# Second layer rebuilt as a pipeline of 32 items, with projections of rounded parts

## The reference, cut to what matters

```python
def shared_kv(x, g_norm, w_kv, g_k):
    kv = rmsnorm(x, g_norm) @ w_kv
    k, v = jnp.split(kv, [KV_WIDTH], axis=-1)
    k = rmsnorm(k.reshape(b, s, SWA_KV_HEADS, SWA_HEAD_DIM), g_k)
    ...    # bands: each block of 128 rows sees itself and the block before

def swa_layer(x, g_norm, w_in, g_q, sinks, w_out, k_band, v_band, bias, mask):
    proj = rmsnorm(x, g_norm) @ w_in
    q, gate = jnp.split(proj, [SWA_Q_WIDTH], axis=-1)
    q = rmsnorm(q.reshape(b, nb, BLOCK, SWA_KV_HEADS, SWA_GROUP, SWA_HEAD_DIM), g_q)
    scores = jnp.einsum('bnqkgd,bnjkd->bnkgqj', q, k_band).astype(jnp.float32)
    scores = scores * (SWA_HEAD_DIM ** -0.5) + bias[None, None]
    scores = jnp.where(mask[None, :, None, None], scores, -jnp.inf)
    m = jnp.maximum(jnp.max(scores, axis=-1, keepdims=True), sink)
    p = jnp.exp(scores - m)
    p = p / (jnp.sum(p, axis=-1, keepdims=True) + jnp.exp(sink - m))
    o = jnp.einsum('bnkgqj,bnjkd->bnqkgd', p.astype(v_band.dtype), v_band)
    o = o.reshape(b, s, SWA_Q_WIDTH) * jax.nn.silu(gate)
    return x + o @ w_out
```

## Time and profile before

| what | value |
|---|---|
| median of three runs | 2690.94 us (2686.0 to 2691.65) |
| profiled execution: span | 2686.3 us |
| profiled execution beside the runs | 0.3 above the lowest, 4.6 below the median; no other time of it is given |
| TensorE busy | 2500.3 us, 93% |
| VectorE busy | 1077.8 us, 40% |
| ScalarE busy | 751.9 us, 28% |
| POOL busy | 211.1 us, 8% |
| first stage | 0 to 936.7 us |
| second stage | 936.7 to 1537.1 us |
| third stage | 1537.1 us to the end |

### The profile page before, as it was taken

The page is one execution under the profiler, slowest core; times in us unless marked ns, Lnnn a source line. Parts: engine busy times, 40 slices in busy tenths (PEclk is TensorE's granted clock), DMA queues, the critical chain, the costliest instruction groups (busy, mean ns, idle before and its releaser), DMA issues. The chain is left out here.

```text
span 2686.3 us, 32568 instructions
## 1 busy us (share of the span) xinstructions
PE 2500.3 (93%) x11482; PEld 1864.2 (69%) x11482; DVE 1077.8 (40%) x2949; ACT 751.9 (28%) x1960; POOL 211.1 (8%) x292
## 2 busy tenths in 40 slices
PE   6999999999899878999999789999999998799998
PEld 5867778677578735555555477777777675688877
DVE  4223122241231134444444234676676767211132
ACT  3121221212220022222222132444444534211131
POOL 0010000100100010000000000001010000000013
PEclk8999999999999988999999888999999999899999
DMA  3111111111261252000001121011111010311112
GB/s 127 49 51 61 39 55 49 51 45 53 78 229 63 74 178 96 9 8 8 8 8 39 44 74 49 26 36 40 55 39 39 25 36 9 113 48 47 47 71 94
DMA packets 77371, 152.32 MB, mean 57 GB/s; under 512 B 6392, under 2 KB 26040, under 8 KB 75584
## 3 DMA queue, kind: packets, MB, share of 16 engines
q1 hardware_dynamic: 66768, 130.65, 13.8%
q10 hardware_dynamic: 9616, 13.81, 1.5%
q0 software_dynamic: 864, 6.29, 0.6%
HBM read 124.46 MB, written 26.27 MB: 56 GB/s over the span
## 5 line engine op out<-in xcount | busy, mean ns | idle before, releaser
L91 PE MATMUL heads_p_ps<-ret_w_second_hi_sb,ret_hT_hi_sb 128*128 128x512 f32 x384 | 161.7, 421 | 1.1 <-DVE ret_w_second_lo_sb L465 1.1
L91 PE MATMUL heads_p_ps<-ret_w_second_lo_sb,ret_hT_hi_sb 128*128 128x512 f32 x384 | 149.9, 390 | 0.0
L91 PE MATMUL heads_p_ps<-ret_w_second_hi_sb,ret_hT_lo_sb 128*128 128x512 f32 x384 | 149.4, 389 | 0.0
L921 PE MATMUL swa_p_ps<-swa_w_o_sb,swa_oT_sb 128*128 128x512 f32 x256 | 118.2, 617 | 0.9 <-DVE swa_oT_sb L1316 0.9
L921 PE MATMUL swa_p_ps<-swa_w_g_sb,swa_xT_sb 128*128 128x512 f32 x256 | 114.4, 600 | 3.9 <-DVE swa_w_g_sb L1343 3.9
L2506 DVE TENSOR_TENSOR mrg_sig_sb<-mrg_b_ps,mrg_sig_sb 128x512 f32<-128x512 f32 x32 | 22.1, 690 | 235.9 <-PE mrg_b_ps L2362 235.9
L2362 PE MATMUL mrg_b_ps<-mrg_w_br_sb,mrg_yT_sb 128*128 128x256 f32 x512 | 115.5, 379 | 0.0
L91 PE MATMUL att_proj_ps<-br_w_second_hi_sb,br_hT_hi_sb 128*128 128x512 f32 x256 | 110.7, 432 | 2.7 <-DVE br_w_second_lo_sb L2008 2.7
L1161 ACT ACTIVATE swa_probs_sb<-swa_probs_sb,swa_max_neg_sb 128x256 f32<-128x256 f32 x128 | 63.4, 496 | 169.9 <-DVE swa_max_neg_sb L1294 169.9
L2362 PEld LDWEIGHTS mrg_b_ps<-mrg_w_br_sb,mrg_yT_sb 128*128 128x128 f32 x512 | 96.5, 190 | 13.6
L1970 ACT ACTIVATE br_x_sb<-br_x_sb,att_max_neg_sb 128x256 f32<-128x256 f32 (+7 forms) x128 | 97.8, 768 | 19.5 <-DVE att_max_neg_sb L2181 19.5
(11 more groups left out here) (393 smaller groups left out, 5830.8 us busy)
## 6 DMA issues: line engine op xcount, KB each, us to landing
early_w_kv_sb<-a_w_blocks SPq DMA_DIRECT2D x28, 1024.0 KB, 5.1
all_w_block_sb<-w_turns SPq DMA_DIRECT2D x12, 2048.0 KB, 9.0
ret_o_dram<-heads_o_gated_sb ACTq DMA_DIRECT2D x32, 256.0 KB, 2.4
ret_out_o_rows_sb<-ret_o_dram POOLq DMA_DIRECT2D x6, 1024.0 KB, 5.2
heads_v_sb<-x SPq DMA_DIRECT2D x8, 512.0 KB, 4.3
all_w_block_sb<-a_w_blocks SPq DMA_DIRECT2D x2, 2048.0 KB
ret_out_x_rows_sb<-x SPq DMA_DIRECT2D x8, 512.0 KB, 5.4
x_dram<-ret_out_x_rows_sb SPq DMA_DIRECT2D x8, 512.0 KB, 2.6
```

The costliest lines, as they stand in the source:

```text
L91: mm = pe.matmul(out, rows[a], w[b], start=(k == 0 and a + b == 0), stop=(k == KT - 1 and b == 1))
L921: mm = pe.matmul(bank[:, 0:cols.stop - cols.start], h[:, k, :], w[:, k, cols], start=(k == 0), stop=(k == KT - 1))
```

## The change

Only the second stage is written anew, with a small part of it moved into the first.

- Work is cut into 32 items: four turns (one quad of heads each) over eight tiles. An item has one projection of 512 columns, 256 for the queries and 256 for the gates of its four heads; `window_blocks` lays the weights out that way. Item n goes through step n+1 (norm), n+2 (scores, maxima, exponentials), n+3 (transposes, values) and n+4 (gate, transposes of the output). All steps are written out; there is no hardware loop.
- The projections use `products` with parts. So normed rows of all eight tiles are kept transposed in two parts (`hT`), made in an opening loop together with all keys and values (`k_all`, `v_all`). Weights are split by `split_high` (ScalarE) and `split_low` (VectorE); the first half of k has two buffers, the second half (`w_second`) one.
- The outputs are stored transposed to DRAM, item by item, loaded again per tile, split, and projected by 16 products of 512 columns, four of them in steps 32 to 35 and twelve after them.
- The gate is x(1 + tanh(x/2)), with the factor 1/2 in the output weights: one tanh on ScalarE and one operation on VectorE. The product of gate and output moves to POOL, and so does the sink's difference.
- In the first tile the half of the band that is masked is left out, so no mask has to be put in and out.
- The product of bucket table and one-hot matrix, and its store, are done in the first stage; the second loads the skewed form and VectorE reverses it with a negative step (`flip_bias`).

```diff
 # first stage
+                if t == 3:
+                    pe.wait_ge(rel_in, 48)
+                    pe.matmul(p_o0[0:SWA_HEADS, 0:EXT], rel, onehot, start=True, stop=True).then_inc(ext_mm, 1)
...
+            act.wait_ge(ext_done, 1)
+            act.dma_start(dram["ext"], ext).then_inc(ext_out, 16)
...
+                if t == 5:
+                    dve.wait_ge(ext_mm, 1)
+                    dve.wait_ge(rel_in, 48)
+                    dve.tensor_tensor(ext, p_o0[0:SWA_HEADS, 0:EXT], ext_mask, ALU.add).then_inc(ext_done, 1)
...
+            dve.wait_ge(ext_out, 16)
 # second stage, TensorE
+            def keys_values(t):
...
+                mm = products(pe, p_kv[t % 2][:, 0:KV_COLS], at_tile(hT, slice(t * P, (t + 1) * P)),
+                              lambda k: [part[:, k, :] for part in w_kv])
+            def project(n, ks):
+                turn, t = divmod(n, TILES)
+                if ks[0] == 0:
+                    at_least(pe, qn_done, n - 1)
+                    at_least(pe, gate_done, n - 1)
+                if t == 0:
+                    pe.wait_ge(w_lo, KT * turn + ks[-1] + 1)
+                mm = products(pe, p_proj[n % 2][:], at_tile(hT, slice(t * P, (t + 1) * P)), lambda k: turn_w(turn, k), ks)
...
+            for s in range(TILES + 2):
+                if s < TILES:
+                    rows(s)
+                if 1 <= s <= TILES:
+                    keys_values(s - 1)
+                if s >= 2:
+                    transpose_keys(s - 2)
+                if s in (5, TILES):
+                    project(s // TILES, range(KT))
+            for n in range(1, ITEMS + AHEAD):
+                def along(ks):
+                    if 2 <= n < ITEMS:
+                        project(n, ks)
+                    elif n >= ITEMS:
+                        output(n - ITEMS, ks)
+                if 2 <= n < ITEMS + 2:
+                    scores(n - 2)
+                along(range(0, 3))
+                if 3 <= n < ITEMS + 3:
+                    transpose_probs(n - 3)
+                along(range(3, 6))
+                if 3 <= n < ITEMS + 3:
+                    values(n - 3)
+                if n <= ITEMS:
+                    transpose_queries(n - 1)
+                if n >= 4:
+                    transpose_out(n - 4)
+                along(range(6, KT))
+            for m in range(AHEAD, len(outputs)):
+                output(m, range(KT))
 # second stage, VectorE, one step
+                if t == 0 and turn < QUADS:
+                    for k in range(HALF, KT):
+                        split_low(turn, k)
...
+                if n >= 4:
+                    norm_out(n - 4)
+                if n <= ITEMS:
+                    query_squares(n - 1)
+                    put_gate(n - 1)
+                if 2 <= n < ITEMS + 2:
+                    bias_max(n - 2)
+                if n <= ITEMS:
+                    norm_queries(n - 1)
+                if 3 <= n < ITEMS + 3:
+                    copy_probs(n - 3)
+                    row_sums(n - 3)
+                if HALF <= t and turn + 1 < QUADS:
+                    split_low(turn + 1, t - HALF)
 # second stage, SyncE
+            for n in range(ITEMS):
+                store_out(n)
+                if n >= LOADS:
+                    load_out(n - LOADS)
+                if n == TILES or n == 2 * TILES:
+                    sp.wait_ge(w_lo, KT * (n // TILES + 1))
+                    sp.dma_start(w_raw[:], kt_view(dram["swa_turns"][n // TILES + 1])).then_inc(w_in, 16)
```

More of the change, by code:

```diff
@@ new lines, in turn_w, with late_w, o_parts, keys_of @@
+        def turn_w(turn, k):
+            return [part[:, k % HALF, :] for part in (w_first[turn % 2] if k < HALF else w_second)]
+        def late_w(k):
+            return [part[:, k, BANK:] for part in hT]
+        def o_parts(t):
+            cols = slice(t % 4 * P, (t % 4 + 1) * P)
+            return [part[:, :, cols] for part in hT]
+        def keys_of(n):
+            t = n % TILES
+            return (0 if t else P), slice(max(t - 1, 0) * P, (t + 1) * P)
+        outputs = [(t, 0) for t in range(4)] + [(t, 1) for t in range(4)]
@@ L851, in window_layer @@
+        for t in (4, 6):
+            outputs += [(t, 0), (t + 1, 0), (t, 1), (t + 1, 1)]
+        AHEAD = 4
+        LOADS = ITEMS - TILES + 2
+        LATE = {1: range(0, 3), 2: range(3, 6), 3: range(6, KT)}
         block = ctx.enter_context(nc.Block())
@@ L959, in transpose_qk @@
                 for g in range(SWA_KV):
[L960 removed]
+                    tr = pe.transpose(p_kv[t % 2][:, KV_COLS + g * P:KV_COLS + (g + 1) * P], kn[:, g].rearrange("p a d -> p (a d)"), ident[:])
                 tr.then_inc(kT_tr, 1)
[L962 to L969 removed]
@@ L1083, in _, with output @@
-            in_blocks(pe, step_pe)
-            last = Place(None, 0, TILES - 1)
-            transpose_out(last)
-            output(last, 0)
-            output(last, 1)
+                pe.wait_ge(og_done, n + 1)
+                at_least(pe, oT_done, n)
+                for m in range(2):
+                    tr = pe.transpose(p_m[:, (2 + m) * P:(3 + m) * P], o_gated[:, n % 2, m * P:(m + 1) * P], ident[:])
+                tr.then_inc(oT_tr, 1)
+            def output(m, ks):
+                t, half = outputs[m]
+                if ks[0] == 0:
+                    at_least(pe, x_added, m - 1)
+                    if m < 2:
+                        pe.wait_ge(qn_done, ITEMS)
+                        pe.wait_ge(gate_done, ITEMS)
+                    pe.wait_ge(o_lo, t + 1)
+                if t == 0:
+                    pe.wait_ge(wo_lo, KT * half + ks[-1] + 1)
+                parts = o_parts(t)
+                mm = products(pe, p_proj[m % 2][:], lambda k: [part[:, k, :] for part in parts],
+                              lambda k: late_w(k) if half else turn_w(QUADS, k), ks)
+                if ks[-1] == KT - 1:
+                    mm.then_inc(y_done, 1)
@@ L1409, in branches_layer @@
+            for m in range(AHEAD - 1, len(outputs)):
+                add_rows(m)
+                if AHEAD <= m < TILES:
+                    out_low(m)
 def branches_layer(nc, ident, dram, w_raw, y_post):
@@ L2597, in head_blocks, with window_blocks @@
     return np.stack(blocks)
+def window_blocks(w_in):
+    width = QUAD * SWA_HD
+    return np.stack([np.concatenate([w_in[:, off + n * width:off + (n + 1) * width] for off in (0, DIM)], axis=1) for n in range(QUADS)])
 def turn_blocks(w_in):
```

985 lines of the change are left out of this document (463 added, 522 removed).

## The result

The changed kernel takes 2621.11 us (median of four runs, 2618.1 to 2623.32) against 2689.02 for the kernel before on the same chip: a ratio of 0.9757, 95% interval 0.9741 to 0.9773. It is faster by 68 us. The forecast was 2563, with a range of 2540 to 2615: the sign came out, the time lies outside the range, and about half of the gain forecast is missing.

A forecast was written before the change was run, and what follows sets the result against it. TensorE, busy 93%, was taken as the bound; second-stage terms summed to 471 against 600.4 (-129), first stage +1, so 2686.3 to 2558, plus 4.6 for the runs' median: 2563, range 2540 to 2615.

The forecast's parts named there:

- A step, 10.0: Second stage's steady pipeline step: TensorE's work takes 10.0 us, other engines stay below that, waits cost nothing.
- The rival with a step of 11.5: Steady steps: longer handovers let the other engines' chain set the step, 45 us more, 2608 in all; chance 0.17.
- The opening, 70 with bounds 55 to 92: Second stage's start to first scores: 10 before transposes, 45 for eight tiles, 11 for two projections, 4 for the chain.
- The half-clock rival: Opening: TensorE at half clock needs 7.8 us a tile, above VectorE's 5.6; 2585 in all; chance 0.14.
- Weight loads, cost at nothing, "at least five steps ahead of use except the last, two ahead": Four weight loads in the second stage: issued early enough to cost nothing; a late one up to 9 us.
- Four changes of weights at 2 each: Steps 8, 16, 24, 32: four splits delay the copy that values wait for, 2 us each, 8 in all.
- Steps 32 to 35 and the output projections, 106 with the tail and the last change: Second stage's end: steps 32 to 35 take 34, twelve other output projections 65.5, add, store and barrier 4.7.
- First-tile items and the first short step: Second stage: four first-tile items lack half their band, -7.5 us; the step without transposes takes 6.5.
- First stage +1: First stage: the bias product and small loads moved there cost 1 us, between 0 and 4.

The follow-up runs named there:

- e3: Changed kernel with ScalarE copying the keys of tile s-3 before scaling the rows of tile s+2 in the opening; 2599.94 us, ratio 0.9677.
- e4: Changed kernel with keys copied first on ScalarE and rows squared before the low parts on VectorE in the opening; 2591.64 us, ratio 0.9648.
- e8: Changed kernel with earlier loads, first output projection awaiting item 30, keys and squares first, plus two of four late splits behind the probabilities copy; 2554.73 us.
- e7: Changed kernel with earlier weight loads, and 8 plain full-precision products for 24 of parts in each of 32 projections; 2630.18 us, ratio 0.9791.

## Why the prediction was off, point by point

The forecast of the stage was 471; the changed kernel's profile has 538.3. The missing 67 us, against its own terms:

- **A step, 10.0**: 9.90. Right, and with it the reading of parts by their starts, the list of TensorE's work in a step, and the view that no other engine sets it. Two small errors cancel in it: the parts with their dearer starts took 5.96 against 5.81, since they follow at 0.23 and not at 0.2275 (the rows that were given for it make 0.225: 0.45 for two), and the other pieces took 3.94 against 4.20. The rival with a step of 11.5 is out.
- **The opening, 70 with bounds 55 to 92**: 100.7, outside the bounds: +31. This is the first step that failed. It was priced by the first stage's 5.6 a tile on the ground of a like load on VectorE. But load did not bound it: the order on ScalarE closed a ring through four engines. The check of steady steps was made by following waits; the opening was priced by analogy. e3 and e4 exchange two pairs of calls, leave all the work, and give 81.2 and 72.8, near the 70; by terms, e4 has 9.5 to the first transposes (forecast 10), 59.0 for tiles and projections (56) and 4.3 for the chain to the first scores (4). The half-clock rival's tiles of 7.8 came out early in the changed kernel (ScalarE's scalings start at 950.32, 957.41, 965.22 and 973.03), but its mechanism is at most a smaller part: it had TensorE busy at half clock as the bound, and here TensorE sat idle for 44.7 of the 100.7.
- **Weight loads, cost at nothing, "at least five steps ahead of use except the last, two ahead"**: the second step that failed. Two of the four were issued at the end of the very step whose first split needs them. The prediction does not show how it counted; the likely slip, not shown, is that it took the item's number in SyncE's condition (8, 16) for a step, and even that would be four steps ahead of the first split. The store of item 8 stands ahead of the load in SyncE's row and is possible only at step 12, where the first split of these weights stands too, and TensorE's step 13 pays for it. I had the price, "a late one at up to 9", and the stalls were 9.0 and 8.6, and 12.5 and 11.5 with the half clock behind them; with 0.6 in the step after the first, +24.6.
- **Four changes of weights at 2 each**: the first three cost 2.7, 1.4 and 1.4, of which 1.2 each is idle before the values, where it was forecast (e8 took them away); the fourth is part of step 32. About right.
- **Steps 32 to 35 and the output projections, 106 with the tail and the last change**: 118.2 (1355.26 to 1473.44), +12. The forecast had no wait for item 31 before the first output projection (6.75, and half clock), nor the 4.5 in four smaller ones before the next projections (0.71, 1.38, 1.38, 1.02).
- **First-tile items and the first short step**: 6.9 saved against 7.5, and the first step 8.9 against 6.5: +3.0 together.
- **First stage +1**: the stage starts 1.6 earlier than before (935.12 against 936.73), and in the other runs of the new first stage between 934.4 and 936.0, so the moved bias costs nothing there that could be seen. Its reversal on VectorE took 0.69 for 1024 columns, half of the 1.4 forecast.

30.7 for the opening, 24.6 for the loads, 12.0 for the end and 3.0 for the short steps, less 2.9 for 29 steps at 9.90 and 0.3 for the three changes of weights: 67.1, and 0.2 is rounding. Outside the stage, 2.6 in the first and 6.4 in the third ran in the kernel's favour.

Of the range: its upper end took single failures (a half-clock opening, a longer step) and no sum of two. With 0 to 18 for the loads that had been costed at nothing, 2615 would have become 2633 and held the time, with the opening still wrong. The forecast's own range is also a little narrower than its bounds: 2563 less 15 and 8 is 2540, and not 2545; VectorE's list for a step adds up to 5.3, and not 5.4. Neither matters to the result.

What stays open: how the 62 us gained divide among the parts of the change. e7 gives 33 to 36 to the parts in 32 of the 48 projections (and to the leaner steps they allow); for the tanh gate, the bias and the order of a pipeline there is no run that undoes each alone. That the tanh gate is covered can be read: its two operations take 0.38 on ScalarE and 0.41 on VectorE for 256 columns, where the reciprocal alone took 3.35 for 512.

## What to carry to other kernels

For every load that a new order moves, write down the step in which it is issued and the step of its first reader, both in the steps of one engine: a condition on an item's number says when the item's store is done, which in a pipeline is several steps later. Follow the waits of the opening and of the last steps as closely as those of the steady step: a pipeline that is bound by TensorE in the middle took 67 us more than forecast, nearly all of it in the opening, at two late loads and in the last steps, and gave 58.5 back when a few calls and two counts changed places. When two versions differ by under half a per cent here, compare the stretch that was changed, not the total.

## What the runs showed of the hardware

- A float32 copy on VectorE with a negative step in its source took 0.69 us for 128 x 1024. The forecast had taken twice that time.

```profile
953.44 0.69 DVE L1288 COPY swa_bias_sb<-swa_probs_sb 128x1024 f32<-128x1024 f32 x1
```

- Products of parts with 256 columns follow each other at 0.12 at full clock and 0.21 at half, 2.9 and 5.1 for 24 (948.84 to 948.96, and 956.08 to 956.29, in the changed kernel's opening).
- POOL's product of 128 x 256 took 0.74, where the forecast had taken 0.6 between bounds of 0.2 and 1.64; its power of 4 columns took 1.01, as forecast.

```profile
1064.22 0.74 POOL L966 TENSOR_TENSOR swa_o_gated_sb<-swa_o_n_sb,swa_gate_sb 128x256 f32<-128x256 f32 x1 [7.73 <-DVE swa_o_n_sb L1363]
1064.92 1.01 POOL L970 TENSOR_TENSOR swa_q_rstd_sb<-swa_q_ms_sb,swa_minus_half_sb 128x4 f32<-128x4 f32 x1
```
